# One gather of both expert rows per column, in one ring of nine slots, and sub-keys stored turned

## The chip, the cores and the metric

The kernel runs on one core of a Trainium2 chip. The time is that of the device, in microseconds (us), from start to end of one execution; smaller is better. The engines named below are PE (matrix products), DVE (vector work), ACT (activations and scaled copies), POOL (it issues the indirect gathers, and does some elementwise work), SP (it issues plain transfers) and the 16 DMA engines that move the data.

## The reference, cut to what matters

One step of a two-layer decoder: layer 0 mixes with an mLSTM, layer 1 with sparse attention, and each is followed by an expert layer (PEER) over all 288 tokens (256 of a prompt, 32 decoded ones). The change is in the expert layer:

```python
def one_block(x):
    q = (x @ w_q).reshape(blk, P_HEADS, P_QDIM)
    s1 = jnp.einsum('nhd,hkd->nhk', q[..., :half], sub_keys[:, 0])
    s2 = jnp.einsum('nhd,hkd->nhk', q[..., half:], sub_keys[:, 1])
    v1, i1 = lax.top_k(s1, P_TOPK)
    v2, i2 = lax.top_k(s2, P_TOPK)
    ...
    gate = jax.nn.softmax(vals, axis=-1)
    u = u_tab[expert]      # (tokens, 8 heads, 16 experts, 1024)
    v = v_tab[expert]
    act = jax.nn.gelu(jnp.einsum('nd,nhkd->nhk', x, u), approximate=False)
    return jnp.einsum('nhk,nhkd->nd', gate * act, v)
```

For each token, 8 x 16 = 128 experts are chosen. Each costs one row of `u_tab` and one of `v_tab`, 1024 fp32 numbers or 4 KB each. The row of u gives a dot product with the token, that gives a weight, and the weighted row of v is added to the token. `sub_keys` are 16 x 128 keys of 128 numbers for each layer.

## The kernel before

**Stages.** A first part (to about 270 us) holds the mLSTM mixer. `weave_stage` is the rest but for the last 12 us (`final_stage`). Its head, `FirstRoute`, finishes layer 0's mixer and finds the experts of the first 128 tokens, half of them, before the loop begins at 376 us.

**The loop over columns.** A column is one of the 128 experts, for 128 tokens at once (token on the partition). Tiles 0 and 1 are the prompt, with 128 columns each. Tile 2, the 32 decoded tokens, is folded four times over the partitions and has 32 columns. Two layers times (128 + 128 + 32) make 576 columns, in six runs. Column i goes through these steps:

- POOL gathers 128 rows of 4 KB from `peer_u` into slot i % 9 of the ring `u` (`load_u`, line 3089), once the dot product of column i - 9 is done (`dotted`).
- POOL gathers the rows of `peer_v` into slot i % 9 of the ring `vrow` (`load_v`, line 3105), once column i - 9 has been applied. It is issued with a lag, `LAG = 10`: just behind `load_u(i + 10)`.
- DVE makes the dot product (line 3177), ACT the Gelu of four columns at once (`GRP = 4`, line 3209). DVE multiplies by the gate, giving `w` (`weigh`, line 3133), two groups of columns later.
- 381 columns are applied by PE: ACT writes a diagonal matrix of the weights (`spread`, line 3202) and PE adds its product with the row of v in PSUM (line 3236, two products of 512 numbers, each recorded as two passes). The other 195 (`shared`) are folded into x by DVE (`fold`, line 3150). `collect` (line 3159) adds PE's sum to x at the end of a run.

**What is woven in.** All the rest of the decoder, the attention layer and the finding of the next experts, is written as side work in "beats". Each engine runs the loop over columns, and after column i it calls `tick`, which runs the side work of two or three beats. So on each engine the order of column work and side work is fixed, and an engine that waits for side work holds up its columns too. POOL's side work is the placing of experts' numbers (`Ranks.place`, lines 1938 to 1948, elementwise on up to 128x1024) and 64 gathers of 8 KB rows of the two caches (lines 1074 and 2172). ACT ticks four slots ahead of its columns, PE's loop nine slots ahead, POOL's nine slots behind its gathers.

**Weights.** SP loads the side work's weights in pieces of 2 MB (128 partitions x 8 x 512 numbers, rows of 2 KB) over the same DMA engines.

**Sub-keys.** They come as (key, head, dimension) and PE turns them by 16 transposes, ACT copies them out, once in `FirstRoute` (`turn_keys`, lines 2712 and 2874) and once in `RouteWork` (lines 1985 and 2046).

## Time and profile before

| | us |
|---|---|
| median of 3 runs | 2577.95 (2577.82 to 2581.94) |
| span of the profiled execution | 2568.0 |
| median less that span | 9.95 |
| POOL busy (61%), 1415 instructions | 1573.5 |
| PE busy (76%) | 1963.6 |
| DVE busy (57%) | 1460.2 |
| ACT busy (28%) | 717.5 |
| DMA: 805.63 MB, mean over the span | 314 GB/s |

The profiled execution is one run with its records on. Its span goes from the first to the last instruction, and what the timed runs have besides (9.95 us) lies outside. An engine's busy time leaves out the time in which it issues, waits or branches. A busy share of a stage says little by itself; the rows below are read stage by stage.

### The profile page before, as it was taken

Reading aid. Unit: us, or ns where it says so; the run is one execution under the profiler, and the core shown is the slowest. Engines: PE = TensorE matmul, PEld = TensorE weight load, DVE = VectorE, ACT = ScalarE, POOL = GpSimd, SP = SyncE. Lnnn points to the kernel's source line nnn. Section 1 sums busy time; section 2 is a strip of 40 time slices with the busy share of each in tenths; the row PEclk is TensorE's granted clock in tenths of the full one; section 3 lists DMA queues with packets and bytes.
Section 4 is the critical chain, followed back from the end, with each engine's and each line's share of the span. In section 5 each row is a group of like instructions: output and inputs, shape, how many; then the busy total and the mean of one; then the engine's idle time right before and its main releaser. Section 6 shows DMA issues by size and latency. Waiting matters only on the chain. (4 is left out here: it accounts for less than half of the span.)

```text
span 2568.0 us, 22709 instructions
## 1 busy us (share of the span) xinstructions
PE 1963.6 (76%) x6982; PEld 973.0 (38%) x6982; DVE 1460.2 (57%) x3278; ACT 717.5 (28%) x1732; POOL 1573.5 (61%) x1415
## 2 busy tenths in 40 slices
PE   5999797696878676987867868976677878759666
PEld 4435565353434233555421234553223333313211
DVE  1025257694465653576774356849438677764653
ACT  1111112685556311331211123411113333302101
POOL 2021027888777775677688667766647666456674
PEclk9975799898899787888988878988788999969879
DMA  6232519977999999999988998898779999899797
GB/s 195 99 137 80 172 36 335 348 294 250 402 406 410 396 402 391 338 314 400 378 319 292 397 385 316 316 400 295 281 280 408 364 381 369 350 320 403 241 367 284
DMA packets 253936, 805.63 MB, mean 314 GB/s; under 512 B 41780, under 2 KB 46392, under 8 KB 244344
## 3 DMA queue, kind: packets, MB, share of 16 engines
q0 software_dynamic: 176496, 673.82, 69.7%
q1 hardware_dynamic: 77176, 130.37, 14.3%
q8 instruction: 57, 0.93, 0.1%
q14 instruction: 63, 0.52, 0.1%
q10 hardware_dynamic: 144, 0.00, 0.0%
HBM read 798.37 MB, written 14.04 MB: 316 GB/s over the span
## 5 line engine op out<-in xcount | busy, mean ns | idle before, releaser
L3236 PE MATMUL g_acc<-g_vrow,g_diag 128*128 128x512 f32 (+1 forms) x1524 | 827.4, 680 | 277.6 <-DMA g_vrow<-in_peer_v_dram,f_idx 157.5
L3105 POOL DMA_INDIRECT g_vrow<-in_peer_v_dram,f_idx x576 | 681.1, 1182 | 330.9 <-issue 148.8
L3177 DVE CUSTOM_DVE_ANT_0 f_u<-f_u,f_h 128x1024 f32<-128x1024 f32 x576 | 708.8, 1247 | 264.2 <-DMA f_u<-in_peer_u_dram,f_idx 223.1
L3089 POOL DMA_INDIRECT f_u<-in_peer_u_dram,f_idx x576 | 655.1, 1137 | 289.5 <-issue 159.3
L3236 PEld LDWEIGHTS g_acc<-g_vrow,g_diag 128*128 128x128 f32 (+1 forms) x1524 | 281.8, 199 | 735.4 <-issue 547.5
L3150 DVE SCALAR_TENSOR_TENSOR x<-g_vrow,g_w,x 128x1024 f32<-128x1024 f32 x195 | 250.3, 1284 | 100.9 <-DMA g_vrow<-in_peer_v_dram,f_idx 92.4
L3202 ACT ACTIVATE g_diag<-const,g_w 128x128 f32<-128x128 f32 (+1 forms) x381 | 132.0, 379 | 201.5 <-DVE g_w L3133 178.6
L1240 PE MATMUL g_side<-g_slab 128*128 128x512 f32 (+3 forms) x288 | 123.4, 568 | 47.0 <-DMA g_slab<-in_nsa_w_in_dram 46.5
L1100 PE MATMUL g_side<-g_slab 128*128 128x512 f32 x256 | 136.1, 615 | 23.3 <-ACT g_slab L1138 20.3
L1938 POOL TENSOR_TENSOR g_slab<-g_slab 128x1024 f32<-128x1024 f32 (+1 forms) x20 | 44.1, 2207 | 133.4 <-DVE g_slab L1897 132.5
L2240 PE MATMUL g_side<-g_cmp_kT,g_q_blk 128*32 128x512 f32 x160 | 87.7, 632 | 43.8 <-DVE g_cmp_kT L2371 29.1
L1138 ACT ACTIVATE g_slab<-g_more 64x256 f32<-64x256 f32 x256 | 96.7, 378 | 69.3 <-PE g_more L1089 66.2
L1138 ACT ACTIVATE g_slab<-g_side 64x256 f32<-64x256 f32 x256 | 96.7, 378 | 68.3 <-PE g_side L1089 65.1
L3209 ACT ACTIVATE g_gelu<-g_dot 128x4 f32<-128x4 f32 x144 | 29.3, 204 | 302.9 <-DVE g_dot L3177 301.4
L290 PE MATMUL mp_acc<-mp_w,hc_h_T 128*128 128x512 f32 (+3 forms) x240 | 90.7, 531 | 0.0
L1240 PEld LDWEIGHTS g_side<-g_slab 128*128 128x128 f32 (+1 forms) x288 | 42.9, 168 | 120.9 <-issue 71.0
L2010 PE MATMUL g_side<-g_slab 128*128 128x128 f32 x512 | 69.4, 299 | 23.4 <-DMA g_slab<-in_peer_w_q_dram 23.4
L2010 PEld LDWEIGHTS g_side<-g_slab 128*128 128x128 f32 x512 | 68.0, 215 | 29.4 <-DMA g_slab<-in_peer_w_q_dram 25.0
L673 POOL COPY mr_qd<-mx_q_T 64x32 f32<-64x32 f32 x16 | 4.7, 294 | 109.3 <-POOLq L153 108.4
L1864 DVE MAX8 g_v<-g_slab 128x8 f32<-128x128 f32 x136 | 29.3, 278 | 74.1 <-ACT g_slab L2033 30.2
L2369 ACT ACTIVATE g_cmp_kT<-g_side 128x512 f32<-128x512 f32 x40 | 23.8, 594 | 155.0 <-PE g_side L2230 155.0
L3209 ACT ACT_TABLE_LOAD x51 | 65.4, 1283 | 1.0
(409 smaller groups left out, 2451.4 us busy)
## 6 DMA issues: line engine op xcount, KB each, us to landing
g_slab<-in_nsa_w_in_dram SPq DMA_DIRECT2D x15, 2048.0 KB, 19.7
g_slab<-in_peer_w_q_dram SPq DMA_DIRECT2D x14, 2048.0 KB, 21.4
mp_w<-in_mlstm_w_in_dram SPq DMA_DIRECT2D x6, 2048.0 KB, 10.0
g_slab<-in_nsa_w_out_dram SPq DMA_DIRECT2D x6, 2048.0 KB, 17.5
f_u<-in_peer_u_dram,f_idx POOLq DMA_INDIRECT x576, 7.8
g_vrow<-in_peer_v_dram,f_idx POOLq DMA_INDIRECT x576, 7.6
g_slab<-in_state_win_kv_dram SPq DMA_DIRECT2D x8, 1024.0 KB, 8.4
out_win_s_dram<-in_state_win_kv_dram SPq DMA_DIRECT2D x1, 8128.0 KB
```

The source lines that it names most:

```text
L290: mm = pe.matmul(acc[q % banks][0:nt, 0:n], M.h_T[:, c, t0:t0 + nt], w[:, j % WRING, c, 0:n], start=(c == 0), stop=(c == DC - 1))
L1100: pe.matmul(self.ps_h[c], self.w1[:, c, pair].rearrange("p f h -> p (f h)"), self.sub_T[:, q % 3], start=(pair == 0), stop=(pair == CSTR / ...
L1138: ins = act.activation(dst, tr[ADH * g2:ADH * g2 + ADH, l], ACT.Copy)
L1240: mm = pe.matmul(S.bank[2 + j % 2][0:n, 0:cols], self.h_T[s][:, c, 0:n], self.ring[s][:, j % 2, c, 0:cols], start=(c == 0), stop=(c == DC ...
L2010: mm = pe.matmul(S.bank[2 + j % 2][:, c * P:(c + 1) * P], self.proj.ring[0][:, j % 2, k, c * P:(c + 1) * P], self.proj.h_T[0][:, k, :], st ...
L3089: pool.indirect_dma_start(u[:, i % RU, :], None, u_table, bass.IndirectOffsetOnAxis(ap=idx[:, col:col + 1], axis=0), element_offset=layer ...
L3105: pool.indirect_dma_start(vrow[:, i % RV, :], None, v_table, bass.IndirectOffsetOnAxis(ap=idx[:, col:col + 1], axis=0), element_offset=lay ...
L3150: dve.scalar_tensor_tensor(out=M.x[:, t, :], in0=vrow[:, i % RV, :], scalar=w[:, g % 2, k:k + 1], in1=M.x[:, t, :], op0=ALU.mult, op1=ALU. ...
L3177: dve.tensor_tensor_reduce(row, row, h[:, t, :], 1.0, 0.0, ALU.mult, ALU.add, dot[:, g % 2, k:k + 1]).then_inc(dotted, 1)
L3202: act.activation(diag[:, q % (2 * GRP), 0:n], base, ACT.Copy, scale=w[:, i // GRP % 2, i % GRP:i % GRP + 1]).then_inc(diag_ready, 1)
L3209: act.activation(gelu[:, g % 2, :], dot[:, g % 2, :], ACT.Gelu).then_inc(gelu_ready, 1)
L3236: mm = pe.matmul(acc[0:n, a, :], diag[:, q % (2 * GRP), 0:n], vrow[:, i % RV, a * 512:a * 512 + 512], start=first and on_pe[i] == on_pe[GR ...
```

## The change

- `peer_u` and `peer_v` are handed to the device as one table `peer_uv` whose rows are a row of u and then the row of v, 8 KB. One gather per column (line 3076 of the new code) brings both into one slot. POOL's lag of ten columns for v is gone.
- The rings are one ring of nine slots of 8 KB per partition, four in the old `u` tensor and five in the old `vrow` tensor. A slot is free for column i + 9 when column i has been applied by PE or folded by DVE; before, the u half was free after its dot product.
- Column 4 waits for `projected` 5 and column 8 for `scored` 4, since their slots hold `FirstRoute`'s weights.
- Groups are two columns. ACT now scales by the gate as well (two copies of 128x1 per group, each with a wait on ACT's own result), and spreads at once. DVE folds column i - 2 right behind the dot product of column i (`BEHIND = 2`). Four groups of dots and of weights are kept, eight diagonals as before.
- ACT's side work runs one slot ahead of its columns, PE's three, POOL's five behind. The same columns are shared as before. The prompt's side work may start four slots earlier (`P + 4` for `P + 2 * GRP`).
- `sub_keys_T` is handed over with the dimension first, so the load writes `keys_T` (8 KB rows) and the transposes and copies are gone.

```diff
-GRP = 4
-RU, RV = 9, 9
+GRP = 2
+LOW, HIGH = 4, 5
+SLOTS_UV = LOW + HIGH
...
-            sp.dma_start(route.keys, I["peer_sub_keys"][1].rearrange("h s k d -> k (h s) d")).then_inc(route.keys_in, 16)
+            sp.dma_start(S.keys_T, I["sub_keys_T"][1]).then_inc(route.keys_in, 16)
...
-    def turn_keys(self, pe, k):
-        for c in range(4):
-            mm = pe.transpose(self.bank[k % 2][:, c * P:(c + 1) * P], self.keys[:, 4 * k + c, :], self.S.M.ident)
-        mm.then_inc(self.keys_turned, 1)
...
-            beat = max(beat, first_beat(COL0[t] + P + 2 * GRP) + 4)
+            beat = max(beat, first_beat(COL0[t] + P + 4) + 4)
...
+    R = SLOTS_UV
+    BEHIND = 2
+    DRING, WRING_UV = 4, 4
+    DIAGS = 8
...
-                for i in range(NU + LAG):
+                for i in range(NU + R - 4):
                     if i < NU:
-                        load_u(i)
-                    if i >= LAG:
-                        load_v(i - LAG)
-                    if i >= RU:
-                        tick(clock, side, i - RU)
...
+                        if i == LOW:
+                            pool.wait_ge(work.first.projected, 5)
+                        if i == R - 1:
+                            pool.wait_ge(work.first.scored, NJ)
+                        if i >= R:
+                            if shared[i - R]:
+                                pool.wait_ge(folded, on_dve[i - R + 1])
+                            else:
+                                pool.wait_ge(applied, on_pe[i - R + 1])
+                        pool.indirect_dma_start(both(i), None, table,
+                                                bass.IndirectOffsetOnAxis(ap=idx[:, col:col + 1], axis=0),
+                                                element_offset=layer * PK * PK * 2 * D).then_inc(landed[i % R], 16)
+                    if i >= R - 4:
+                        tick(clock, side, i - (R - 4))
...
-                    dve.tensor_tensor(w[:, g % 2, :], gelu[:, g % 2, :], gate[:, col:col + GRP], ALU.mult
-                                      ).then_inc(w_ready, 1)
...
+                        if i >= BEHIND and shared[i - BEHIND]:
+                            fold(i - BEHIND)
+                        if s and i == starts[s] + 3:
+                            collect(s - 1)
                         tick(clock, side, i)
...
+                def weigh(g):
+
+                    col = groups[g][3]
+                    act.wait_ge(dotted, GRP * (g + 1))
+                    act.activation(gelu[:, g % 2, :], dot[:, g % DRING, :], ACT.Gelu).then_inc(gelu_ready, 1)
+                    act.wait_ge(gelu_ready, g + 1)
...
+                    for k in range(GRP):
+                        ins = act.activation(w[:, g % WRING_UV, k:k + 1], gelu[:, g % 2, k:k + 1], ACT.Copy,
+                                             scale=gate[:, col + k:col + k + 1])
...
+                    act.wait_ge(scaled.sem, scaled.n)
+                    act.wait_ge(w_ready, g + 1)
...
-                for slot in range(2 * GRP + 1):
+                for slot in range(3):
                     tick(clock, side, slot)
...
+                        pe.wait_ge(landed[i % R], 16 * (i // R + 1))
+                        pe.wait_ge(diag_ready, q + 1)
+                        for a in range(2):
+                            mm = pe.matmul(acc[0:n, a, :], diag[:, q % DIAGS, 0:n], row(i, 1)[:, a * 512:a * 512 + 512],
+                                           start=i == opens[s], stop=i == closes[s])
+                        mm.then_inc(applied, 1)
+                    tick(clock, side, i + 3)
...
+    rows["sub_keys_T"] = np.transpose(inputs["peer_sub_keys"], (0, 4, 1, 2, 3)).reshape(2, P, HH, P)
+    rows["peer_uv"] = np.concatenate([inputs["peer_u"], inputs["peer_v"]], axis=-1)
```

POOL, early in the loop of columns, where the placing of experts (1938 to 1944) begins between gathers; before:

```order
L3105 DMA g_vrow<-in_peer_v_dram,f_idx 128x1024
L1938 TENSOR_TENSOR g_slab<-g_slab 128x1024
L3089 DMA f_u<-in_peer_u_dram,f_idx 128x1024
L3105 DMA g_vrow<-in_peer_v_dram,f_idx 128x1024
L1942 TENSOR_TENSOR g_slab<-g_slab 128x64x8
```

The same place now (`f_u` and `g_uv` are the two halves of the one ring):

```order
L3076 DMA g_uv<-in_peer_uv_dram,f_idx 128x2048 x2
L1939 TENSOR_TENSOR g_slab<-g_slab 128x1024
L3076 DMA g_uv<-in_peer_uv_dram,f_idx 128x2048
L1943 TENSOR_TENSOR g_slab<-g_slab 128x64x8
L1943 TENSOR_TENSOR g_slab<-g_slab 128x64x4
```

Two issues with 4 KB rows per column have become one with 8 KB rows. The elementwise operations of the placing are the same and still come one step at a time between the columns.

DVE, in the same stage, with the sorting of scores (1864 to 1885) as side work; before:

```order
L3177 ISA f_u,g_dot<-f_u,f_h 128x1024
L3177 ISA g_dot 128x1
L1864 MAX g_slab<-g_slab 128x8 x4
L1866 MAX_INDEX g_ci<-g_slab 128x8 x2
L3177 ISA f_u,g_dot<-f_u,f_h 128x1024
L3177 ISA g_dot 128x1
L3133 TENSOR_TENSOR g_w<-g_gelu,f_gate 128x4
L3150 SCALAR_TENSOR_TENSOR x<-g_vrow,g_w,x 128x1024
```

Now:

```order
L1869 MATCH_REPLACE g_slab<-g_slab 128x256 x4
L3119 ISA f_u,g_dot<-f_u,f_h 128x1024
L3119 ISA g_dot 128x1
L3094 SCALAR_TENSOR_TENSOR x<-f_u,g_w,x 128x1024
L1865 MAX g_slab<-g_slab 128x8 x4
```

The weighing has left DVE, and a fold stands directly behind a dot product, two columns behind its own.

ACT, in the prompt's window attention (1688 to 1696) as side work; before:

```order
L1688 ACTIVATE g_slab<-g_side,g_slab 128x128 x4
L3209 ACT_TABLE_LOAD
L3209 ACTIVATE g_gelu<-g_dot 128x4
L3202 ACTIVATE g_diag<-const,g_w 128x128
L1696 ACTIVATE g_slab<-g_side 128x512
```

Now:

```order
L1689 ACTIVATE g_slab<-g_side,g_slab 128x128 x4
L3145 ACT_TABLE_LOAD
L3145 ACTIVATE g_gelu<-g_dot 128x2
L3150 ACTIVATE g_w<-g_gelu,f_gate 128x1 x2
L3165 ACTIVATE g_diag<-const,g_w 128x128
L1697 ACTIVATE g_slab<-g_side 128x512
```

The diagonal written behind a Gelu was an earlier group's and is now that group's own. In the whole program ACT has 117 table loads before and 135 now.

## Rows read from the trace of the kernel before

**Rows 1.** The page: busy us by engine; DMA queues with packets, MB, share.

```profile
PE 1963.6 (76%) x6982; PEld 973.0 (38%) x6982; DVE 1460.2 (57%) x3278; ACT 717.5 (28%) x1732; POOL 1573.5 (61%) x1415
...
q0 software_dynamic: 176496, 673.82, 69.7%
q1 hardware_dynamic: 77176, 130.37, 14.3%
```

**Rows 2.** Stretches: busy us (and instructions) by engine; granted clock, DMA share, GB/s.

```profile
376.00:650.00 274.00, 206.64 (x882) 123.05 (x881) 181.12 (x545) 143.18 (x353) 221.28 (x197) 0.90 0.85 308
650.00:950.00 300.00, 239.80 (x761) 115.63 (x759) 175.99 (x285) 145.00 (x384) 237.79 (x205) 0.90 1.02 403
950.00:1250.00 300.00, 235.17 (x947) 145.25 (x948) 168.89 (x344) 74.37 (x199) 193.07 (x167) 0.83 0.98 365
1250.00:1400.00 150.00, 101.55 (x208) 32.05 (x207) 95.55 (x262) 24.57 (x65) 122.33 (x109) 0.89 0.86 313
1400.00:1750.00 350.00, 280.26 (x1108) 158.12 (x1107) 207.29 (x416) 88.52 (x219) 227.53 (x199) 0.86 0.97 361
1750.00:1900.00 150.00, 95.30 (x205) 31.59 (x204) 82.80 (x232) 23.49 (x54) 90.02 (x86) 0.80 0.77 273
1900.00:2400.00 500.00, 390.66 (x1480) 153.69 (x1479) 346.67 (x717) 144.81 (x277) 315.55 (x273) 0.89 0.95 364
2400.00:2552.00 152.00, 98.36 (x185) 25.82 (x184) 74.47 (x124) 14.86 (x58) 111.23 (x104) 0.83 0.87 321
```

**Rows 3.** Timeline of POOL, 1351 to 1359: start, duration, idle before and releaser.

```profile
1352.87 1.55 POOL L3089 DMA_INDIRECT f_u<-in_peer_u_dram,f_idx  x1 [0.30 <-issue]
1354.72 0.94 POOL L3105 DMA_INDIRECT g_vrow<-in_peer_v_dram,f_idx  x1 [0.30 <-issue]
```

**Rows 4.** Groups of instructions: count; busy us, mean ns; idle before, releasers.

```profile
L3105 POOL DMA_INDIRECT g_vrow<-in_peer_v_dram,f_idx x576 | 681.1, 1182 | 330.9 <-issue 148.8 <-PE g_acc L3236 102.5 <-DVE x L3150 79.6
L3177 DVE CUSTOM_DVE_ANT_0 f_u<-f_u,f_h 128x1024 f32<-128x1024 f32 x576 | 708.8, 1247 | 264.2 <-DMA f_u<-in_peer_u_dram,f_idx 223.1 <-ACT g_gelu L3209 29.2 <-DVE g_cmp_v L2521 4.1
L3209 ACT ACTIVATE g_gelu<-g_dot 128x4 f32<-128x4 f32 x144 | 29.3, 204 | 302.9 <-DVE g_dot L3177 301.4
L3209 ACT ACT_TABLE_LOAD x51 | 65.4, 1283 | 1.0
L995 ACT ACTIVATE g_ss<-g_ss 128x1 f32<-128x1 f32 (+1 forms) x9 | 1.8, 203 | 53.2 <-DVE g_ss L976 53.1
```

**Rows 5.** Transfers of the page: count, KB each, median us to landing.

```profile
g_slab<-in_nsa_w_in_dram SPq DMA_DIRECT2D x15, 2048.0 KB, 19.7
...
f_u<-in_peer_u_dram,f_idx POOLq DMA_INDIRECT x576, 7.8
```

**Rows 6.** The gathers of 8 KB rows, line 2172: issue times, then issue to landing.

```profile
L2172 POOL DMA_INDIRECT g_slab<-in_cache_sel_kv_dram,f_quarter_idx x32: 933/1032/1981, 1906.6 to 2172.0; - x32
...
DMA to landing us min/median/max: 7.1/9.0/11.9
```

**Rows 7.** Waits by total: engine, line, releaser; us, times, longest.

```profile
DVE g_slab L1637 <- ACT g_slab L1616: 49.5, 2, 27.1
DVE x L3159 <- PE g_acc L3236: 49.0, 3, 24.5
PE g_side L1240 <- DMA g_slab<-in_nsa_w_in_dram: 46.5, 7, 14.4
PE g_side L1449 <- DMA g_slab<-in_nsa_cmp_w_dram: 40.9, 2, 23.0
DVE g_slab L1310 <- ACT g_slab L1278: 40.2, 7, 15.3
```

**Rows 8.** The turning of the sub-keys on PE before the loop, line 2712.

```profile
L2712 PE MATMUL g_side<-const,g_cmp_kT x16: 272/273/328, 300.0 to 303.7; 128*128 128x128 f32 x16
```

**Rows 9.** Timeline, the last gathers of u and v, and PE's last run.

```profile
2526.64 0.94 POOL L3089 DMA_INDIRECT f_u<-in_peer_u_dram,f_idx  x1 [0.30 <-issue]
...
2534.02 19.08 PE L3236 MATMUL g_acc<-g_vrow,g_diag 128*32 128x512 f32 x44 [0.66 <-DMA g_vrow<-in_peer_v_dram,f_idx]
```

215 lines of the change are left out of this document (71 added, 144 removed).

## The prediction

> **What bounds the kernel now.** I read the stretches first [rows 2], then POOL's timeline in one of them [rows 3], then the groups and waits [rows 4, 7]. The chain of waits is of no use here: it is followed back only through the last stage.
>
> No engine's busy share on the page is near full [rows 1], but POOL's busy time leaves out what it needs between issues. In the timeline one gather takes 0.94 us when nothing holds it, the next comes 0.30 us later, and the releaser is "issue", so POOL waited for nobody [rows 3]. With 0.30 us added for each instruction, POOL's stretches are [rows 2]: 376 to 650, 221 + 197 x 0.30 = 280 of 274 us; 650 to 950, 299 of 300; 1250 to 1400, 155 of 150; 2400 to 2552, 142 of 152. There POOL is full. In the others it is not: 243 of 300, 287 of 350, 116 of 150 and 397 of 500. The second thing to see is what the DMA engines carry. From 650 to 950 it is 403 GB/s at a share of 1.02, which is the most of any stretch. In the other three full stretches of POOL it is 308, 313 and 321 GB/s at 0.85 to 0.87: half-idle transfers behind a busy issuer. DVE waits 223 us for rows of u in all [rows 4]. So POOL bounds three stretches (576 us together), DMA and POOL share a fourth, and in the other 1300 us the side work's own dependences and DMA together leave 361 to 365 GB/s (273 from 1750 to 1900).
>
> **What the change removes.** 576 of 1152 gather issues go. Each costs 0.94 + 0.30 = 1.24 us at least, and 1.18 + 0.30 = 1.48 us on the mean of line 3105 [rows 4]. The surplus over 0.94 is the 1.55 us kind [rows 3]. So POOL loses 576 x 1.24 = 714 us or more. The bytes stay the same. What is an issue of 8 KB rows worth? The cache gathers are exactly that, 1.03 us at the median, and they land after 9.0 us [rows 6], where a 4 KB one lands after 7.8 us [rows 5]. So the doubled gather costs POOL as much as a single one.
>
> POOL is then at most 60% busy in its full stretches. What is late next? PE has 207 of 274 us, 102 of 150 and 98 of 152 there; DVE 181, 96 and 74 [rows 2]. DMA at 403 GB/s would need 209, 117 and 121 us. So DMA is next, but the side work's order has never let it be full in stages like these. I take the mean of the three long stretches in which POOL is not full, (300 x 365 + 350 x 361 + 500 x 364) / 1150 = 363 GB/s:
>
> - 376 to 650: 274 x 308 = 84.4 MB, at 363 GB/s 232 us, -42.
> - 1250 to 1400: 47.0 MB, 129 us, -21.
> - 2400 to 2552: 48.8 MB, 134 us, -18.
> - 1750 to 1900: 273 GB/s, but POOL has 34 us free and the side work's chain holds it. At 363 GB/s it would be 113 us. I take a fifth of the 37 us, -8.
> - The end: from the issue of the last u gather (2526.6) to the end of PE's run (2553.1) are 26.5 us, since ten v gathers come behind it [rows 9]. Now the last gather brings both: 9.0 to landing [rows 6], 1.2 for the dot product, 0.2 Gelu, 0.4 scalings, 0.8 diagonals, about 2 on PE, 13.6 us. Half of the 13 us is already in the line above, -6.
> - Sub-keys: PE turns them from 300.0 to 303.9 us, alone, with the token's transposes behind [rows 8]. The norm they would wait for takes about half of that, -2. The second set lies beside columns, 0. The loads (8 KB rows for 512 B ones) 0.
>
> Sum -97.
>
> **What 8 KB rows do to the DMA engines.** q0 needs 0.697 x 2568 x 16 / 176496 = 162 ns per packet of 3.82 KB, q1 76 ns per 1.69 KB [rows 1]. A line through both has 40 ns per KB and 8 ns per packet, so one packet of 8.2 KB instead of two of 4.1 saves 2.2%. Over the 1450 us with a share of 0.95 or more [rows 2], of which columns carry three quarters of the bytes (604 of 806 MB), that is at most 24 us, at least nothing. I take -12.
>
> **Relief elsewhere.** In the 1150 us where POOL is not full it is still an in-order issuer, at 76 to 82%. A quicker reissue is worth between 0 and 1150 x (1 - 363/403) = 114 us. I take -10, near the low end, since landing and side work hold those stages.
>
> **What it adds.** ACT gets 144 more Gelus of 0.20 us, 576 scalings of 0.20 us (a copy of 128x1 takes 203 ns) and 18 table loads of 1.28 us [rows 4]: 29 + 117 + 23 = 169 us, 0.3 us per column. ACT is at 28%, at 48% in its busiest stage from 650 to 950. The cover is there; 144 weighings of DVE go for it. New is who waits: a fold stands two columns behind its dot product, and behind it on DVE are the next dot product and the side work. ACT's chain (table load 1.3, Gelu 0.2, scalings 0.4) takes 1.9 us, and two dot products 2 x 1.3 = 2.6 us, so it is just covered unless ACT is in side work. The bounds are 0 and 195 x 1.3 = 250 us (every fold waits for a table load). The ring adds the second new wait: POOL issues column i + 9 only when i is applied. A slot is held for landing (9 us [rows 6]), then for the dot product, the weighing, the diagonal and PE's products, some 10 us with the wait for the second of a pair. Nine slots at 2176 / 576 = 3.8 us per column are 34 us, so some 15 us of stall and side work are ridden out, where the two rings rode more. Both together +15, near the low end. The waits of columns 4 and 8 at the start are met while the first gathers move, 0.
>
> -97 - 12 - 10 + 15 = -104 us. The profiled span would be 2568 - 104 = 2464; with the 9.95 us outside it the forecast is 2474, I say **2475 us**.
>
> **The rivals.**
>
> *A, weights starve (2550 us).* Side work's weights come in 2 KB rows on q1, beside gathers. A piece of 2 MB lands after 19.7 us [rows 5], 106 GB/s. If engines took a packet from each queue in turn, q1 would get 1.69 / (1.69 + 3.82) = 31% of some 390 GB/s, 120 GB/s, which fits. With 8.2 KB packets it would be 17%, 67 GB/s, and a piece lands 11.6 us later. PE waits nine times for such pieces (46.5 us in 7, 40.9 in 2 [rows 7]); 9 x 11.6 = 104, of which the emptying ring gives some back, +75. For it: the fit. Against: most pieces are loaded well ahead.
> The Trainium skill, "DMA: Bandwidth & Descriptors", section on queues, rings and completion order, says that each engine goes round the queues packet by packet; by that rule A is what must happen to weights beside a full gather queue, and this trace's 106 GB/s agrees with it.
>
> *B, the ring is too short (2645 us, slower).* The price is in the long stalls of PE and DVE: 49.5 + 49.0 + 46.5 + 40.9 + 40.2 = 226 us in 21 waits of up to 27 us [rows 7]. Before, the u ring and the lag of v let gathers run on through much of them; now none is issued once nine columns are unapplied, and after each stall DMA starts empty. If three quarters of 226 us are lost anew, +170. It ends slower once the loss passes 104 us, nearly half. For it: one slot now waits for three engines. Against: the count above leaves 15 us of slack.
>
> *C, everything opens (2385 us).* The loop moves about 760 MB from 376 to 2552 us. At 95% of 403 GB/s, 383, that takes 1984 of 2176 us, -192. For it: 650 to 950 runs at 403 already. Against: 1900 to 2400 has POOL at 79% and reaches only 364.
>
> *D, nothing (2578 us).* DMA would be the bound throughout and POOL full by chance. Against: 308 GB/s at 0.85.
>
> **How the numbers follow.** Forecast 0.62 (2420 to 2545), C 0.14, A 0.12, B 0.10, D 0.02. The range goes from 2380, through the middle of C, to 2570, past A; B is left out. A measurement can tell 0.2% from no change (5 us). Faster: 0.62 + 0.14 + 0.12 = 0.88; same 0.02; slower 0.10.
>
> **What the new profile would show.** POOL's gathers: 576 of about 1 us, POOL busy below 1000 us. 376 to 650 shorter by some 40 us, at 360 GB/s or more. POOL's idle time goes to waits for PE's and DVE's applied columns. Issue to landing between 8 and 15 us. Were A right, weights would land after 28 us or more. Were B right, DMA's share would fall below 0.85 in 950 to 1250 and 1900 to 2400, with POOL waiting for PE. The forecast is wrong if folds wait for ACT by more than 50 us in all, or if the stretches with POOL free change by more than 3% either way.

## The result, and the profile after

The changed kernel takes 2570.2 us (median of 20 runs, 2563.2 to 2583.3), the kernel before in the same comparison 2577.9 us (20 runs). The ratio is 0.997, 95% interval 0.9956 to 0.9983. It is faster by 8 us where 103 were forecast, and 0.2 us above the top of the range (2380 to 2570 us). The profiled span went from 2568.0 to 2569.9 us, at a mean granted clock of 0.863 and 0.861.

The page after (busy us by engine; the queues), beside [rows 1]:

```profile
PE 1970.7 (77%) x6950; PEld 981.6 (38%) x6950; DVE 1468.7 (57%) x3134; ACT 916.4 (36%) x2462; POOL 942.9 (37%) x839
...
q0 software_dynamic: 93552, 673.78, 66.0%
q1 hardware_dynamic: 76408, 130.37, 14.2%
```

POOL lost 631 us of busy time and the program did not get shorter. The stretches after (busy us and instructions by engine; clock, DMA share, GB/s), beside [rows 2]:

```profile
376.00:650.00 274.00, 226.93 (x937) 131.61 (x935) 196.22 (x538) 173.63 (x463) 167.36 (x145) 0.93 0.88 344
650.00:950.00 300.00, 232.39 (x728) 113.89 (x728) 171.10 (x258) 166.06 (x477) 126.11 (x99) 0.89 0.99 403
950.00:1250.00 300.00, 239.18 (x971) 143.60 (x969) 184.69 (x372) 108.91 (x314) 111.08 (x93) 0.89 0.93 365
1250.00:1400.00 150.00, 116.08 (x248) 35.54 (x248) 100.20 (x235) 42.08 (x137) 84.73 (x70) 0.89 0.94 377
1400.00:1750.00 350.00, 270.28 (x1032) 162.72 (x1033) 201.32 (x386) 117.80 (x318) 111.95 (x94) 0.80 0.83 320
1750.00:1900.00 150.00, 102.94 (x233) 34.08 (x231) 83.97 (x223) 34.29 (x96) 63.70 (x59) 0.82 0.71 274
1900.00:2400.00 500.00, 364.07 (x1403) 143.01 (x1403) 309.45 (x593) 179.75 (x400) 149.59 (x138) 0.87 0.88 342
2400.00:2552.00 152.00, 101.31 (x193) 28.26 (x192) 95.85 (x175) 37.22 (x138) 72.65 (x65) 0.85 0.89 360
```

Where POOL had been full the bytes flow faster: 308 to 344, 313 to 377 and 321 to 360 GB/s. In two of the other stretches they flow slower: 361 to 320 and 364 to 342. So the change gains and loses in different places. To see where, I took from both traces the start of the dot product of each column (576 columns; the five pieces are columns 0 to 128, and so on). The last dot product's start to the end of the span is another 35.4 us before and 20.8 after.

```
us                0-128  128-304  304-416  416-512  512-575
before            475.7    619.3    457.8    396.5    203.1
changed           454.5    605.1    484.0    433.4    191.2
difference        -21.2    -14.2    +26.2    +36.9    -11.9
```

With the end's -14.6 that is 62 us gained, and 63 us lost between columns 304 and 512. Columns 416 to 512, called the decode piece below, run beside the side work of decoding, from about 1930 to 2350 us. Each row of pieces is read from one profiled execution, and executions of one kernel lie up to 35 us apart (20 us for the changed kernel), so a difference of a few us in one piece says little, and pieces need not add up to the difference of the medians. All that follows asks what took the 63 us. Two views suggest different causes. The waits of the whole run (engine, line, releaser: us, times, longest):

```profile
POOL g_uv L3076 <- PE g_acc L3193: 512.3, 144, 25.1
POOL f_u L3076 <- PE g_acc L3193: 383.9, 116, 17.3
```

POOL's gathers now wait 896 us for a column to be applied by PE (102.5 us before [rows 4]) and another 141 us for one to be folded (79.6 before). That speaks for **theory R**: the joint ring is too short, a slot being held from its gather to its apply. The waits between 1900 and 2400 us, of PE, DVE and POOL:

```profile
PE g_side L2240 <- ACT g_slab L2378: 36.7, 12, 5.1
PE g_side L2238 <- ACT g_slab L2378: 17.9, 8, 5.2
PE g_side L2252 <- ACT g_slab L2367: 13.5, 7, 3.4
...
DVE g_cmp_kT L2351 <- PE g_more L2210: 68.5, 21, 6.1
...
POOL g_slab L2152 <- PE g_side L2252: 71.0, 10, 10.5
POOL g_slab L2152 <- PE g_side L2258: 27.1, 3, 9.0
```

These are waits of side work for side work: PE for ACT 68 us (before some 12), DVE for PE's line 2210 68.5 us (before 51), POOL's cache gathers for PE 98 us (before none). That speaks for **theory S**: the order in which each engine mixes side work and columns got worse. The timeline shows one such wait being made (start, duration, what, idle before and releaser; ACT, then PE, then POOL):

```profile
2141.16 1.28 ACT L3145 ACT_TABLE_LOAD   x1
2144.76 0.20 ACT L3145 ACTIVATE g_gelu<-g_dot 128x2 f32<-128x2 f32 x1 [2.32 <-DVE g_dot L3119]
2144.99 0.48 ACT L3150 ACTIVATE g_w<-g_gelu,f_gate 128x1 f32<-128x1 f32 x2
...
2146.50 0.57 ACT L2367 ACTIVATE g_slab<-g_side 128x512 f32<-128x512 f32 x1
...
2147.12 1.44 PE L2252 MATMUL g_side<-g_slab 128*64 128x256 f32 x8 [2.43 <-ACT g_slab L2367]
...
2153.23 0.94 POOL L2152 DMA_INDIRECT g_slab<-in_cache_sel_kv_dram,f_quarter_idx  x1 [9.04 <-PE g_side L2258]
2154.47 0.94 POOL L2152 DMA_INDIRECT g_slab<-in_cache_sel_kv_dram,f_quarter_idx  x1 [0.30 <-issue]
2155.72 0.94 POOL L3076 DMA_INDIRECT g_uv<-in_peer_uv_dram,f_idx  x1 [0.30 <-issue]
```

ACT stands before a Gelu whose dot product is not there. Its side step 2367 is queued behind it, PE's 2252 waits for that, and POOL, held up by PE's side work, issues no column gather from 2144.2 to 2155.7 us, though the slot of the next one was free at 2145.9. ACT's 2.3 us is only the start of POOL's 9 us: from 2147.1 on PE is busy with side work nearly all the time.

### The profile page after: what moved, and what is told of

It is laid out like the page before. It is cut to its first block and busy times, and to the rows that moved or that the text cites. A ratio compares the mean times of both kernels' runs of the same rounds, so it can differ in the third digit from the quotient of the medians.

```text
span 2569.9 us, 23064 instructions
## 1 busy us (share of the span) xinstructions
PE 1970.7 (77%) x6950; PEld 981.6 (38%) x6950; DVE 1468.7 (57%) x3134; ACT 916.4 (36%) x2462; POOL 942.9 (37%) x839
## 5 line engine op out<-in xcount | busy, mean ns | idle before, releaser
L3076 POOL DMA_INDIRECT g_uv<-in_peer_uv_dram,f_idx x320 | 389.6, 1217 | 642.0 <-PE g_acc L3193 512.3
L3193 PE MATMUL g_acc<-g_uv,g_diag 128*128 128x512 f32 (+1 forms) x848 | 451.7, 670 | 110.8 <-ACT g_diag L3165 109.1
L3119 DVE CUSTOM_DVE_ANT_0 g_uv<-g_uv,f_h 128x1024 f32<-128x1024 f32 x320 | 405.2, 1271 | 212.1 <-DMA g_uv<-in_peer_uv_dram,f_idx 204.4
L3076 POOL DMA_INDIRECT f_u<-in_peer_uv_dram,f_idx x256 | 299.6, 1170 | 491.9 <-PE g_acc L3193 383.9
L3119 DVE CUSTOM_DVE_ANT_0 f_u<-f_u,f_h 128x1024 f32<-128x1024 f32 x256 | 325.0, 1276 | 180.6 <-DMA f_u<-in_peer_uv_dram,f_idx 174.9
L3193 PE MATMUL g_acc<-f_u,g_diag 128*128 128x512 f32 (+1 forms) x676 | 356.4, 661 | 69.3 <-ACT g_diag L3165 51.7
L3193 PEld LDWEIGHTS g_acc<-g_uv,g_diag 128*128 128x128 f32 (+1 forms) x848 | 156.9, 197 | 353.3 <-issue 336.4
L3193 PEld LDWEIGHTS g_acc<-f_u,g_diag 128*128 128x128 f32 (+1 forms) x676 | 125.4, 198 | 254.8 <-issue 234.1
L1241 PE MATMUL g_side<-g_slab 128*128 128x512 f32 (+3 forms) x288 | 128.9, 589 | 55.0 <-DMA g_slab<-in_nsa_w_in_dram 52.4
L3094 DVE SCALAR_TENSOR_TENSOR x<-g_uv,g_w,x 128x1024 f32<-128x1024 f32 x108 | 138.4, 1281 | 7.6 <-ACT g_w L3150 7.6
L3150 ACT ACTIVATE g_w<-g_gelu,f_gate 128x1 f32<-128x1 f32 x576 | 138.2, 287 | 9.4
## 6 DMA issues: line engine op xcount, KB each, us to landing
g_slab<-in_nsa_w_in_dram SPq DMA_DIRECT2D x15, 2048.0 KB, 19.1
```

What stands on the lines that cost most here:

```text
L1241: mm = pe.matmul(S.bank[2 + j % 2][0:n, 0:cols], self.h_T[s][:, c, 0:n], self.ring[s][:, j % 2, c, 0:cols], start=(c == 0), stop=(c == DC ...
L3076: pool.indirect_dma_start(both(i), None, table, bass.IndirectOffsetOnAxis(ap=idx[:, col:col + 1], axis=0), element_offset=layer * PK * PK ...
L3094: dve.scalar_tensor_tensor(out=M.x[:, t, :], in0=row(i, 1), scalar=w[:, i // GRP % WRING_UV, i % GRP:i % GRP + 1], in1=M.x[:, t, :], op0=A ...
L3119: dve.tensor_tensor_reduce(row(i, 0), row(i, 0), h[:, t, :], 1.0, 0.0, ALU.mult, ALU.add, dot[:, g % DRING, k:k + 1]).then_inc(dotted, 1)
L3150: ins = act.activation(w[:, g % WRING_UV, k:k + 1], gelu[:, g % 2, k:k + 1], ACT.Copy, scale=gate[:, col + k:col + k + 1])
L3193: mm = pe.matmul(acc[0:n, a, :], diag[:, q % DIAGS, 0:n], row(i, 1)[:, a * 512:a * 512 + 512], start=i == opens[s], stop=i == closes[s])
```

## The experiments

The edits are against the changed kernel. Four numbers describe an order: how many columns ACT's side work is **ahead** of its columns, how many PE's is ahead, how many columns POOL's is **behind** its gathers, and how many DVE's **fold** is behind its dot product. The changed kernel has 1, 3, 5 and 2. The kernel before had 4, 9 and 9, with folds by groups of four. (Its 4 is counted from the Gelu. Its diagonals were written a group later, so its side work stood eight columns ahead of them.) Ratios are to the kernel before, with 95% intervals.

```
run                 ACT PE POOL fold  ratio (interval)         0-128 128-304 304-416 416-512 512-575
changed              1   3   5    2   0.9970 (0.9956, 0.9983)  454.5   605.1   484.0   433.4   191.2
r8                   1   3   4    2   1.0030 (1.0010, 1.0050)  459.7   618.2   483.0   436.2   188.7
split2               1   3   5    2   1.0175 (1.0143, 1.0206)  479.9   630.0   484.1   431.4   205.7
tworing              1   3   5    2   1.0346 (1.0322, 1.0370)  514.4   607.2   488.5   426.3   208.7
poollate             1   3   8    2   1.0030 (1.0005, 1.0055)  469.3   602.7   478.4   444.9   189.3
pool3                1   3   3    2   1.0068 (1.0044, 1.0092)  463.9   609.4   491.0   432.9   191.2
pe4p4                1   4   4    2   1.0071 (1.0043, 1.0100)  452.3   623.4   476.4   457.6   187.4
act3                 3   3   5    2   1.0564 (1.0527, 1.0600)  536.8   627.1   482.0   450.0   196.1
a3p3                 3   3   3    2   1.0625 (1.0588, 1.0662)  547.0   634.8   508.9   447.7   196.1
a3b3                 3   3   5    3   1.0417 (1.0380, 1.0454)  530.9   635.5   497.2   423.8   195.4
a3p4pe4              3   4   4    2   0.9915 (0.9877, 0.9953)  458.7   613.1   470.9   424.8   187.9
b3                   1   3   5    3   1.0066 (1.0044, 1.0087)  453.2   609.8   480.8   457.3   191.0
b3a3p4pe4            3   4   4    3   0.9785 (0.9754, 0.9816)  456.3   623.5   465.8   393.9   188.8
b4a4pe5p4            4   5   4    4   0.9922 (0.9894, 0.9949)  472.5   630.0   455.2   416.4   182.2
b3a3p4pe4_r8         3   4   4    3   0.9878 (0.9838, 0.9918)  471.6   626.0   465.3   398.9   185.4
b3a3p4pe4_split      3   4   4    3   1.0024 (0.9991, 1.0057)  486.3   653.5   466.3   394.9   200.9
dw_a1_p4_pe5         1   5   4    -   1.0027 (1.0004, 1.0049)  464.5   623.4   476.9   432.7   185.1
dw_a3_p4_pe5         3   5   4    -   1.0214 (1.0164, 1.0265)  517.8   641.8   480.9   408.8   186.3
sw304               1/3 3/4 5/4  2/3  0.9744 (0.9712, 0.9776)  453.4   600.4   460.3   395.8   187.4
```

### A slot fewer, the gathers apart, the rings apart

**r8**, eight joint slots:

```diff
-LOW, HIGH = 4, 5
+LOW, HIGH = 4, 4
```

> The changed kernel with eight joint slots in place of nine (the number of the last slots goes from five to four), nothing else. Theory R (the joint ring is too short: a slot is held from its gather to its apply, some 43 us in the decode stretch, and the ring then lets through one column per hold divided by nine): with eight slots the same hold gives 5.4 us per column in place of 4.8 us where the ring decides, and column 576 comes later: 30 to 80 us slower than the changed kernel, 2600 to 2650 us, POOL's gathers waiting over 1000 us for the applied and folded columns (896 us with nine). Theory S (the new order of the consumers and POOL's own side work cost the time, not the number of slots): within 10 us of the changed kernel, 2560 to 2580 us, with the waits of the gathers only moved.

15 us slower than the changed kernel, between what the two theories asked for; but the place decides. The pieces lose 18 us in columns 0 to 304. From 304 to 512, where the 63 us were lost, a slot fewer costs 2 us. There a slot was held 39.8 us on the mean with nine slots (columns 416 to 512, gather's issue to apply) and 35.1 with eight: 4.4 us per column and slot in both. The pace stayed and the hold shrank with the ring, so the hold followed the pace and did not set it. (In columns 0 to 128 it shrank too, from 28.9 to 26.0, and there the pace did slow, by 5 us in all. So it is the pace that tells.) The waits are the sign of a full ring, not of its price: for applied and folded columns together they are 1087 us with eight slots and were 1037 with nine. The transfers of the changed kernel in 1900 to 2400 us say the same (count, median us to landing):

```profile
g_uv<-in_peer_uv_dram,f_idx POOLq DMA_INDIRECT x61, 9.3
f_u<-in_peer_uv_dram,f_idx POOLq DMA_INDIRECT x51, 9.4
```

A column's rows are there after 9 us, and its dot product starts 25.6 us after the issue (mean of columns 416 to 512). The rows lie some 16 us waiting for DVE, which is in side work or waits for it.

**split2**, the merged gather alone undone:

```diff
-                        pool.indirect_dma_start(both(i), None, table,
+                        for part, table in enumerate((u_table, v_table)):
+                            pool.indirect_dma_start(row(i, part), None, table,
...
-                        dve.wait_ge(landed[i % R], 16 * (i // R + 1))
+                        dve.wait_ge(landed[i % R], 32 * (i // R + 1))
```

> The changed kernel with the merged gather undone alone: each column's slot is filled by two gathers of 4 KB per partition from the two tables, one behind the other, in place of one of 8 KB. Ring, holds and the consumers' order stay. If merging is what brought the 40 us and 21 us of 376-650 and 1250-1400 us back, both come back as losses here (POOL busy again over 1350 us; 2610 to 2650 us). Theory R adds that POOL's second issue per column (0.94 us and 0.30 us) is only paid where POOL did not wait for the ring, so in the decode stretch (1900-2400 us) nothing changes. If the gain before column 304 came from somewhere else (sub-keys, order), this kernel stays within 15 us of the changed kernel, 2555 to 2585 us.

1.0175 against 0.997: the merged gather is worth 2.05%, 53 us. By the pieces it is -25, -25, 0, +2 and -15 us (63 together, as the profiled execution of split2 was 9 us above its median). It pays in the pieces that hold the stretches where POOL had been full, and nowhere else, as forecast. The halved rows come back together with the 576 issues here, and no run takes the two apart. It follows too that the rest of the change costs 45 us, for with the gathers apart it is 1.75% slower than the kernel before.

**tworing**, two rings of nine 4 KB slots, u free at its dot product, v asked for four columns later:

```diff
+                        if i >= R:
+                            pool.wait_ge(dotted, i - R + 1)
...
+                        load(i, 0, u_table, landed)
+                    j = i - LAG
...
+                        load(j, 1, v_table, v_landed)
```

> The changed kernel's consumers and schedule, but two rings of nine 4 KB slots, each with its own gather as before: the u half is free again at its dot, the v half is asked for four columns behind its u half. So merging and joint slots are undone, the new order of dots, weighing, folds and POOL's side work kept. Theory R: without the joint slot the waits of 896 us go and the decode stretch comes back to the 364 GB/s of the kernel before, so the time is that of the kernel before, 2560 to 2590 us, with POOL again the bound in 376-650 us, and its column 304 about 35 us later than in the changed kernel but the last column no later. Theory S: the new order still costs its 30 to 60 us while the merged gather's gain is gone: 2610 to 2650 us.

Slower than forecast by either theory, for a reason of its own: POOL's gathers in 650 to 950 us take 1.25 to 1.30 us where split2's take 1.01 to 1.09 (see the last section). Against R it speaks all the same: without a joint slot columns 304 to 512 still take 915 us, as in split2 (916) and the changed kernel (917), and 854 before. Neither merging nor the joint slot lost the 63 us. These three share the consumers' order, and also the stored sub-keys, the groups of two and the earlier start of the prompt's side work; the runs below, which keep those and move only the order, tell which it was.

### One lead at a time

**poollate** and **pool3**, POOL's side work eight and three columns behind its gathers (the first edit; pool3 has 3 in place of R - 1):

```diff
-                for i in range(NU + R - 4):
+                for i in range(NU + R - 1):
...
-                    if i >= R - 4:
-                        tick(clock, side, i - (R - 4))
+                    if i >= R - 1:
+                        tick(clock, side, i - (R - 1))
```

> The changed kernel with POOL's side work (its gathers of cache rows and its small steps) put eight columns behind its gathers in place of five. The 98 us in which POOL's cache gathers waited for PE's side work with column gathers queued behind them should shrink. Theory S (head-of-line waits in POOL's order cost the decode stretch): 15 to 35 us faster than the changed kernel, 2535 to 2555 us. Theory R (the hold of the slots bounds, and POOL's side wait only overlaps it): within 8 us of the changed kernel, 2562 to 2578 us; if side work that is later on POOL holds back PE and DVE instead, slower.

> The changed kernel with GpSimd's side work three columns behind its gathers in place of five, so that a side step of slot s needs column s-6 applied and no longer s-4. Eight behind (poollate) cost some 13 us against five. If that loss comes from the coupling of GpSimd's side steps to the applied columns, three behind gains: 5 to 15 us faster than the changed kernel, 2558 to 2568 us, decode stretch (column 416 to 512) under 430 us. If GpSimd's side steps then only wait longer for TensorE with more column gathers queued behind them, it is 0 to 20 us slower, its waits of lines 1075 and 2152 for TensorE over 98 us.

15 and 25 us slower than the changed kernel: neither brought the gain, and pool3 lies just past the 0 to 20 us of its second case, with the waits of lines 1075 and 2152 for PE at 185 us. With eight behind, the 98 us of waits of the cache gathers are gone, and the decode piece is 445 us where 397 were hoped for. So these waits were a symptom. The six kernels so far with ACT at 1, PE at 3 and the fold at 2 (changed, r8, split2, tworing, poollate, pool3) take 915 to 924 us for columns 304 to 512, whatever POOL and the rings do.

**act3**, ACT's side work three ahead:

```diff
-                tick(clock, side, 0)
+                for slot in range(3):
+                    tick(clock, side, slot)
...
-                        tick(clock, side, GRP * g + k + 1)
+                        tick(clock, side, GRP * g + k + 3)
```

> The changed kernel with ScalarE's side work (its part of the attention and routing work) three columns ahead of its column work in place of one; in the kernel before it ran four ahead. Nothing else. In the trace of the changed kernel TensorE waits in 1900-2400 us for ScalarE's side steps (lines 2378, 2367: 36.7, 17.9 and 13.5 us = 68 us, 5 us before the change) and GpSimd's cache gathers wait for TensorE's side steps behind that (98 us). Theory S (the side chain is held up by this lead): the 68 us go below 25 us, the decode stretch (column 416 to 512) goes from 433 us back towards 397 us, and the time falls by 20 to 40 us: 2535 to 2555 us. Theory R (the ring's hold bounds, the side waits lie beside it): within 8 us of the changed kernel, 2562 to 2580 us.

The clearest miss: 153 us slower. The waits of act3 (whole run) show two prices. DVE's folds now wait for weights, 8.8 us in the changed kernel, and ACT waits for PE's compression steps:

```profile
DVE x L3094 <- ACT g_w L3151: 331.1, 80, 23.1
...
ACT g_slab L1139 <- PE g_side L1090: 71.7, 34, 4.8
ACT g_slab L1139 <- PE g_more L1090: 60.3, 34, 4.1
```

ACT has two more columns of side work before its weighing and stands as far ahead as PE itself (3 and 3). It waits for PE's side step, and an engine that waits in side work holds its own columns up. The wait it was meant for did go, from 68 to 20 us in 1900 to 2400 us, and the decode piece was no shorter for it (450 us).

**a3p3**, act3 and pool3 together:

```diff
-                        tick(clock, side, GRP * g + k + 1)
+                        tick(clock, side, GRP * g + k + 3)
...
-                    if i >= R - 4:
-                        tick(clock, side, i - (R - 4))
+                    if i >= 3:
+                        tick(clock, side, i - 3)
```

> Both edits: ScalarE's side work three columns ahead (one in the changed kernel) and GpSimd's three behind its gathers (five). Theory S: the two waits are one chain, ScalarE's side step, then TensorE's, then GpSimd's gather of cache rows; with both loosened the decode stretch comes to 400 us and below, and the whole to 2525 to 2550 us, faster than each of the two edits alone. Theory R: 2560 to 2580 us as the changed kernel.

It gave 1.0625, worse than either: the two do not make one chain as I had put it.

### Leads together

**a3p4pe4** and **pe4p4**, PE four ahead and POOL four behind, the first with ACT three ahead:

```diff
-                        tick(clock, side, i - (R - 4))
+                        tick(clock, side, i - 4)
...
-                    tick(clock, side, i + 3)
+                    tick(clock, side, i + 4)
```

> ScalarE's side work three columns ahead, GpSimd's four behind, and TensorE's four ahead in place of three. TensorE one column further ahead of its applies takes side work sooner, but runs further ahead of ScalarE's and VectorE's: Theory S: as a3p3 within 10 us, 2525 to 2555 us, if the lead between ScalarE and TensorE is what counts (one column here, none in a3p3) then 5 to 15 us slower than a3p3. Theory R: 2560 to 2580 us.

> The changed kernel with TensorE's side work four columns ahead of its applies (three) and GpSimd's four behind its gathers (five), ScalarE's left at one. The kernel with these two and ScalarE three ahead took 0.9915 of the kernel before, and ScalarE three ahead alone 1.056. If TensorE's lead is what helps and ScalarE's lead only costs (its weighing is then late for VectorE's folds, 331 us), this is better still: 2535 to 2552 us, VectorE's folds waiting under 30 us for ScalarE. If the two leads must go together (ScalarE's side steps wait for TensorE's and the other way round), it is no better than the changed kernel: 2565 to 2600 us.

With ACT at one: 1.0071. With ACT at three: 0.9915, the first gain. So neither move helps alone, and three ahead on ACT, which cost 153 us beside PE's three, gains 40 beside PE's four (with POOL at four in place of five). PE's waits for ACT's side steps in 1900 to 2400 us fell from 68 to 28 us, DVE's for PE's line 2210 from 68.5 to 23.9. But the folds wait for weights there now, and the decode piece is only 9 us shorter than the changed kernel's (a3p4pe4, 1900 to 2400 us):

```profile
DVE x L3094 <- ACT g_w L3151: 45.1, 17, 5.5
DVE g_cmp_kT L2351 <- PE g_more L2210: 23.9, 16, 2.9
```

**b3a3p4pe4** and **b3**, the fold three columns behind, in that order and in the changed kernel's:

```diff
-    BEHIND = 2
+    BEHIND = 3
```

> ScalarE three ahead, GpSimd four behind, TensorE four ahead, and VectorE's fold three columns behind its dot in place of two. VectorE's folds waited 176 us for ScalarE's weighing in the kernel with the fold two behind. If that wait costs time, it falls below 80 us and the time by 10 to 25 us against that kernel (0.9915 of before): 2530 to 2550 us. If the ring's hold counts more (a folded slot is held one column longer), it is level or up to 10 us slower: 2555 to 2570 us.

> The changed kernel with VectorE's fold three columns behind its dot in place of two, nothing else. In the changed kernel VectorE's folds waited only 8.8 us for ScalarE's weighing, so if the fold's place counts only together with ScalarE's side work further ahead, this is within 8 us of the changed kernel (0.997 of before), with the decode stretch (column 416 to 512) at 425 to 440 us. If the fold's place alone brings the decode stretch back to 394 to 400 us, it is 25 to 40 us faster: 0.982 to 0.988 of before.

In the order with the leads mended it takes the decode piece from 424.8 to 393.9 us (396.5 before the change), and the whole to 0.9785. The wait of the folds over the whole run fell from 176.0 to 40.5 us:

```profile
DVE x L3094 <- ACT g_w L3151: 40.5, 14, 15.8
```

Alone it is 25 us slower than the changed kernel, which neither expectation had: its folds had hardly waited (8.8 us), and a folded slot is held longer. POOL's waits for folded columns went from 141 to 340 us. Its bytes of 1900 to 2400 us are those of the kernel before again (b3a3p4pe4, the stretch as above):

```profile
1900.00:2400.00 500.00, 378.31 (x1460) 148.30 (x1460) 342.65 (x676) 190.38 (x435) 179.69 (x162) 0.89 0.92 363
```

**a3b3**, ACT three ahead and folds three behind, PE's and POOL's leads as in the changed kernel:

```diff
-    BEHIND = 2
+    SWITCH = 0
+    AHEAD = ((3, 5, 3, 3), (3, 5, 3, 3))
...
-                        tick(clock, side, GRP * g + k + 1)
...
+                    ticker.upto(GRP * g + GRP + lead(GRP * g, 0))
```

(`AHEAD` holds the leads of ACT, POOL and PE and the place of the fold, before and from column `SWITCH`; `upto` ticks as far as the lead asks.)

> The changed kernel with ScalarE's side work three columns ahead and the folds three columns behind, TensorE's lead at three and GpSimd's at five. ScalarE three ahead alone cost 150 us: 331 us of folds waiting for ScalarE's weighing, and some 130 us more of ScalarE waiting for TensorE's side steps (line 1139). If the folds were the way by which it cost, this is near the best order, 2525 to 2560 us. If ScalarE's waits for TensorE's side steps at equal leads are what costs, the loss stays above 100 us, 2660 to 2710 us, and TensorE one column ahead of ScalarE is the part that counts.

1.0417: 38 us better than act3, 163 worse than with PE and POOL moved by one column. ACT's waits for PE at line 1139 stay (141 us, 56 in b3a3p4pe4). So most of ACT's price is in PE's and POOL's leads. No run moved PE alone. But POOL at three (a3p3) and at five (act3, a3b3) beside ACT 3 and PE 3 lose alike in columns 0 to 128, and the waits that go are ACT's for PE, so PE's lead is the likelier part (more under dw_a3_p4_pe5 below).

**b4a4pe5p4**, a step further on ACT, PE and the folds:

```diff
-    BEHIND = 2
+    BEHIND = 4
...
-                    tick(clock, side, i + 3)
+                    tick(clock, side, i + 5)
```

> The order loosened one step more on each engine: ScalarE four ahead, TensorE five, folds four behind, GpSimd four behind. If waits between the engines' side work still cost time, another 5 to 20 us off the best order: 0.971 to 0.977 of before. If the hold of the joint slot now bounds (a folded slot is held one column longer, TensorE's applies come behind more side work), 5 to 30 us slower: 0.980 to 0.990.

0.9922, level with a3p4pe4. It is the best of all in columns 304 to 416 and 512 to 575 and loses 6 to 23 us to b3a3p4pe4 in the other three (POOL waits 97 us for folded columns in 1900 to 2400 us, 63 in b3a3p4pe4). That is a little slower than either expectation. A hold of the joint slot that now bounds would fit, but it is read from a wait alone, and no run took a slot away in this order.

### Ring and merging in the better order

**b3a3p4pe4_r8** and **b3a3p4pe4_split** repeat r8 and split2 on b3a3p4pe4:

```diff
-LOW, HIGH = 4, 5
+LOW, HIGH = 4, 4
```

```diff
+                        for part, table in enumerate((u_table, v_table)):
+                            pool.indirect_dma_start(row(i, part), None, table,
```

> The best order found (ScalarE three ahead, GpSimd four behind, TensorE four ahead, folds three behind; 0.9785 of before) with eight joint slots in place of nine. Theory R, if the ring bounds once the order is mended: 30 to 60 us slower than with nine, 0.990 to 1.002 of before. If the order was the cause and nine slots are about enough: as in the changed kernel, where the ninth slot was worth some 14 us: 5 to 20 us slower, 0.980 to 0.987.

> The best order found with the merged gather undone, two gathers of 4 KB per partition into each joint slot. In the changed kernel's order this cost 53 us (1.0175 against 0.997 of before). If the merged gather's worth is that of GpSimd's 576 second issues where GpSimd bounds, it is the same here within 15 us, 0.994 to 1.003 of before, and the loss lies in columns 0 to 128, 128 to 304 and 512 to 575, not in the decode stretch.

The ninth slot is worth 0.93%, 24 us, a little more than the 5 to 20 us expected of it, and again not mainly in columns 304 to 512 (5 us of it there). Merging is worth 2.4%, 62 us: 30, 30, 0, 1 and 12 by the pieces. So 53 to 62 us is the price of the second gather per column in this program, in both orders.

### Weighing on DVE again

**dw_a1_p4_pe5** and **dw_a3_p4_pe5**, one multiplication per group on DVE, the folds behind it, ACT spreading the group before:

```diff
+                    dve.tensor_tensor(w[:, g % WRING_UV, :], gelu[:, g % 2, :], gate[:, col:col + GRP], ALU.mult
+                                      ).then_inc(w_ready, 1)
...
-                        ins = act.activation(w[:, g % WRING_UV, k:k + 1], gelu[:, g % 2, k:k + 1], ACT.Copy,
-                                             scale=gate[:, col + k:col + k + 1])
```

> Weighing goes back to VectorE, one multiplication of a group of two, a group behind its dots, with the folds behind it; ScalarE then spreads the weights of the group before. The 576 scalings of 287 ns leave ScalarE (165 us by the earlier trace), 288 short operations go to VectorE, and each slot is held some two columns longer until its apply; TensorE's side work five ahead, GpSimd's four behind. If ScalarE's part in the chain of a column is what costs (gelu, scaling, spreading behind side work), 15 to 35 us faster than the changed kernel, 2535 to 2555 us. Theory R (the hold of the joint slot decides): two columns more of hold are 20 to 60 us slower, 2590 to 2640 us.

> The same with ScalarE's side work three columns ahead in place of one, near the order of the kernel before. With the weighing off ScalarE its side work no longer holds up VectorE's folds through the scalings, only through gelu: if that was why three ahead cost 150 us in the changed kernel, it costs under 30 us here against one ahead, and the decode stretch (column 416 to 512) comes to 400 to 415 us: 2530 to 2570 us. Theory R: as the kernel with one ahead, 2590 to 2640 us.

1.0027 and 1.0214. Without the scalings on ACT and with ACT one ahead, the decode piece stays at 432.7 us and the whole is 15 us slower than the changed kernel; a slot is held some two columns longer, so the two effects aren't apart, and both totals (2589 and 2639 us) lie at or in the range that theory R gave. With ACT three ahead the decode piece fell to 408.8, but columns 0 to 304 lost 72 us more. So taking the scalings off ACT does not make its lead cheap. ACT writes its diagonals a group later in these two kernels, so dw_a3_p4_pe5's side work stands five columns ahead of them, and PE's stands at five too, with POOL's at the four of the good orders. ACT's waits at line 1139 are 139 us again:

```profile
ACT g_slab L1139 <- PE g_side L1090: 82.1, 29, 15.4
ACT g_slab L1139 <- PE g_more L1090: 57.0, 27, 2.7
```

The four orders in which ACT, counted from its diagonals, stands level with PE (act3, a3p3, a3b3, dw_a3_p4_pe5) have 132 to 144 us of this wait and take 518 to 547 us for columns 0 to 128. With PE one ahead (a3p4pe4, b3a3p4pe4, b4a4pe5p4) it is 45 to 56 us, and those columns take 456 to 473. The wait by itself is not the price: the kernel before had 131 us of it too (its line 1138) and took 476.

### Each order where it is good

**sw304**, the changed kernel's order up to column 304, b3a3p4pe4's from there:

```diff
+    SWITCH = 304
+    AHEAD = ((1, 5, 3, 2), (3, 4, 4, 3))
...
-                    tick(clock, side, i + 3)
+                    ticker.upto(i + 1 + lead(i, 2))
```

> The changed kernel's own order up to column 304, the best order found (ScalarE three ahead, TensorE four ahead, GpSimd four behind, folds three behind) from column 304 on. If what each order costs is tied to the side work that runs at that place, the stretches add up: columns 0-128 454.5 us and 128-304 605.1 us of the changed kernel, 304-416 465.8 us, 416-512 393.9 us and 512-575 188.8 us of the best order, 2108 us against 2128 us of the best order alone, so 20 us less, 2500 to 2512 us or 0.969 to 0.973 of before. If the transfers only move (a lead won before column 304 is eaten by a DMA that is full later), 2515 to 2535 us.

2509.7 us, 0.9744 (0.9712 to 0.9776): the lowest here, 2.6% under the kernel before and 2.3% under the changed one; its interval overlaps that of b3a3p4pe4. The pieces add up to 2097 us where 2108 were expected, but the profiled execution was the fastest of six, 9 us under the median. Each order brought its pieces with it, so an order's price belongs to the side work beside which it runs. Its stretches 1400 to 1750 and 1900 to 2400 us:

```profile
1400.00:1750.00 350.00, 261.05 (x1052) 153.89 (x1052) 228.97 (x497) 122.43 (x332) 128.56 (x106) 0.85 0.88 339
1900.00:2400.00 500.00, 379.57 (x1439) 148.58 (x1438) 345.35 (x647) 186.64 (x432) 185.75 (x167) 0.90 0.92 362
```

## Why the prediction was wrong

The sign was right, the size was not. In the loop's first 304 columns the sum had -63 and the trace gives -35; in columns 304 to 512 it had -8 and the trace gives +63; from 512 to the end it had -24 and the trace gives -26.5. (The -12, -10 and +15 of the sum have no place of their own.)

**What bounds the kernel** was read rightly: POOL bounds three stretches, and these are where split2 gives the time back. As rates the sums for two of them held: 377 GB/s in 1250 to 1400 us and 360 in 2400 to 2552, with 363 forecast. For 376 to 650 it was 344, and there the first gathers of the joint ring come in jerks (the dot product of column 16 is 20 us late). A rate in one stretch is not time saved, though. Columns 0 to 304 gained 35 us where the sum had 42 + 21. Why the other 28 us did not come is not settled: no order brought them (the shortest seen are 452 us for columns 0 to 128 and 600 for 128 to 304), and of the ring it is only known that the ninth slot was worth 18 us there; no run has a tenth. 1750 to 1900 stayed at 274 GB/s, 0 in place of -8. The end gave -15 in all, with 13 in the sum. The loop's first gather came 1.2 us earlier with the sub-keys turned (2 forecast), but its first dot product did not (380.9 us, 380.2 before).

**The step that failed** is the last term, "Both together +15", together with "Relief elsewhere ... -10". I costed of the new order only two waits, the fold for ACT and the ring. The folds waited 8.8 us in all, as forecast. But the diff also moves the side work of three engines against their columns: ACT from four ahead to one, PE from nine to three, POOL from nine behind to five. I counted these moves at nothing, though they are what the stages without a full POOL rest on. Columns 304 to 512 lost 63 us, and leads and folds alone take 58 and 61 of these back (b3a3p4pe4 and sw304 by their pieces). The rest of the miss is the 28 us above: even sw304, at 2509.7, stays 35 us over the forecast of 2475. The prediction's own test, POOL-free stretches changing by more than 3%, is what fired: 361 to 320 and 364 to 342 GB/s.

**The ring** was mis-sized too. I put the hold at some 20 us; the mean is 28.9 us in columns 0 to 128. Nine slots at 3.55 us per column are 32 us there, so there is no slack of 15 us, and the ninth slot is worth 15 to 24 us. Rival B stays refuted in its size: DMA's share is 0.93 and 0.88 in its two stretches, not under 0.85, and its place, the long stalls, didn't lose (950 to 1250 us runs at 365 GB/s as before). The stretch that did fall under 0.85, 1400 to 1750 us at 0.83, it had not named, and columns 304 to 416, in which most of that stretch lies, come back to 466 and 460 us with the same nine slots (b3a3p4pe4, sw304).

**Rival A** was half there. Over the run a 2 MB piece of weights lands after 19.1 us (19.7 [rows 5]). In the full stretch, 650 to 950 us, it went from 21.1 to 28.8 (before, then after):

```profile
g_slab<-in_nsa_w_in_dram SPq DMA_DIRECT2D x5, 2048.0 KB, 21.1
```

```profile
g_slab<-in_nsa_w_in_dram SPq DMA_DIRECT2D x5, 2048.0 KB, 28.8
```

That agrees with the rule of the Trainium skill, "DMA: Bandwidth & Descriptors", section on queues, rings and completion order, that engines go round the queues packet by packet. But PE's waits for these pieces grew from 46.5 to 52.4 us only, and those for the other weights of [rows 7] fell from 40.9 to 30.5, so the +75 was not there.

**ACT** got 199 us more, with 169 forecast. A scaling takes 287 ns where I took 203. I called that row of [rows 4] a copy; its line 995 is a square root of 128x1. The 576 scalings are 138.2 us in all, since two overlap:

```profile
L3150 ACT ACTIVATE g_w<-g_gelu,f_gate 128x1 f32<-128x1 f32 x576 | 138.2, 287 | 9.4
```

No run shows a price for it: dw_a1_p4_pe5, without the scalings, is no faster. **The larger rows**: from 650 to 950 us the best slices of 7.5 us reach 424 GB/s, 416 before, which is the 2% forecast. But the stretch as a whole carried 403 GB/s in both, so no run shows the -12 us as time.

## What to carry to other kernels

In a kernel that weaves two kinds of work on in-order engines, the distance by which each engine runs one ahead of the other is a cost term of its own, as large as the main one. A diff that moves PE's `tick` from nine columns ahead to three is not bookkeeping; write down every lead before and after, and ask at each stage who then waits for whom. The leads must be changed together: each one that was moved alone (POOL's, ACT's, the fold's) cost 15 to 153 us here, all together gained 48. And a long wait for a ring's slot doesn't say that the ring is short: take a slot away and see where time is lost.
